# A float32 encoder layer on one core: 512-wide projection chunks, a ring of ten weight slices, an output projection summed by mixer, projection spread over all of the attention

## The reference

```python
h = x @ w_in                                   # 1024 -> 3328 columns, split below
qa, ka, va, ga, qb, kb, vb, gb = split(h)      # 512 512 512 512 | 512 128 128 512
# mixer A: 8 heads, rotary, sum of three dilated windows by a mask of log counts
# mixer B: 8 query heads on 2 key/value heads, q and k RMS-normalised, axial rotary
out_a = dilated_attention(rope(qa), rope(ka), va) * silu(ga)
out_b = attention(axial_rope(rms(qb)), axial_rope(rms(kb)), vb) * silu(gb)
f = concat(out_a, out_b) @ w_out
y = layer_norm(2 ** 0.25 * x + f, ln_g, ln_b)
```

## Time and profile before

| what | us |
|---|---|
| median of 3 runs (lowest, highest) | 476.59 (476.21, 477.52) |
| span of the profiled execution | 474.6 |
| PE busy, share of the span | 438.0, 92% |
| weight loads of PE | 413.2, 87% |
| DVE busy | 301.4, 64% |
| POOL busy | 248.1, 52% |
| ACT busy | 230.7, 49% |

### The profile page before, as it was taken

How to read it: one execution, slowest core, us unless ns; L and a number is a source line. 1 busy time by engine, 2 the same in 40 slices (tenths; PEclk the granted TensorE clock), 3 DMA queues, 4 the chain that set the end, 5 groups by cost and what they waited for, 6 DMA issues and landing times.

```text
span 474.6 us, 8965 instructions
## 1 busy us (share of the span) xinstructions
PE 438.0 (92%) x3292; PEld 413.2 (87%) x3292; DVE 301.4 (64%) x826; ACT 230.7 (49%) x519; POOL 248.1 (52%) x340
## 2 busy tenths in 40 slices
PE   1999979998899999999999999999999789999990
PEld 1999969987799999998899999999888678999990
DVE  1543675339987788664577877855586777433664
ACT  3332113335456565666565565655675876121222
POOL 1126953795554746334346565653543773454664
PEclk9999989999899999999999999999999989999997
DMA  6611212110200101102010010110200136231222
GB/s 237 255 45 52 71 35 74 39 46 23 68 23 23 46 23 36 56 24 66 14 54 23 24 46 24 40 51 23 68 1 23 44 111 245 88 95 42 78 100 89
DMA packets 23291, 30.00 MB, mean 63 GB/s; under 512 B 1872, under 2 KB 19408, under 8 KB 23248
## 3 DMA queue, kind: packets, MB, share of 16 engines
q1 hardware_dynamic: 22816, 29.30, 19.0%
q10 hardware_dynamic: 432, 0.13, 0.1%
HBM read 26.28 MB, written 3.15 MB: 62 GB/s over the span
## 4 chain that ended last, share of the span: by engine, by line
PE 66%; POOL 10%; DVE 10%; issue 7%; ACT 3%; DMA 2%; SPq 1%; ACTq 0%; DVEq 0%; POOLq 0%
PE bank L504 15%; PE bank L505 15%; PE bank L506 15%; PE bank L465 9%; PE bank L593 6%; POOL scr L1062 3%; DVE prob L870 2%; PE bank L551 2%; PE bank L552 2%; DMA h<-x_prompt 2%; DVE tmp_s L796 1%; POOL tanh L1048 1%; ACT prob L707 1%; DVE p_lo L878 1%; POOL w_lo L1032 1%
## 5 line engine op out<-in xcount | busy, mean ns | idle before, releaser
L504 PE MATMUL bank<-w_hi,t_lo 128*128 128x256 f32 x576 | 168.2, 292 | 1.9 <-DVE nmax L870 0.8
L506 PE MATMUL bank<-w_hi,t_hi 128*128 128x256 f32 x576 | 164.0, 285 | 0.0
L505 PE MATMUL bank<-w_lo,t_hi 128*128 128x256 f32 x576 | 163.9, 285 | 0.0
L504 PEld LDWEIGHTS bank<-w_hi,t_lo 128*128 128x128 f32 x576 | 111.5, 194 | 3.1 <-DVE nmax L870 1.0
L505 PEld LDWEIGHTS bank<-w_lo,t_hi 128*128 128x128 f32 x576 | 111.6, 194 | 0.1
L506 PEld LDWEIGHTS bank<-w_hi,t_hi 128*128 128x128 f32 x576 | 111.3, 193 | 0.0
L1032 POOL TENSOR_TENSOR w_lo<-raw,w_hi 128x512 fp32r<-128x512 f32 x52 | 67.2, 1302 | 59.2 <-ACT w_hi L659 59.1
L1113 POOL TENSOR_SCALAR prob<-prob,den 128x512 f32<-128x512 f32 (+1 forms) x96 | 60.5, 635 | 68.6 <-DVE den L899 68.5
L707 ACT ACTIVATE prob<-prob,nmax 128x512 f32<-128x512 f32 (+1 forms) x96 | 62.3, 649 | 54.1 <-DVE nmax L870 53.6
L878 DVE TENSOR_TENSOR p_lo<-bank,p_hi 128x512 fp32r<-128x512 f32 x80 | 54.8, 685 | 3.0 <-ACT p_hi L716 2.2
L659 ACT ACTIVATE w_hi<-raw 128x512 fp32r<-128x512 f32 x62 | 37.6, 622 | 34.6 <-DMA raw<-w_in 17.4
(11 more groups left out here) (97 smaller groups left out, 784.3 us busy)
## 6 DMA issues: line engine op xcount, KB each, us to landing
raw<-w_in SPq DMA_DIRECT2D x50, 256.0 KB, 2.8
raw<-w_out SPq DMA_DIRECT2D x16, 256.0 KB, 2.9
h<-x_prompt SPq DMA_DIRECT2D x7, 512.0 KB, 6.8
h<-x_sample SPq DMA_DIRECT2D x4, 512.0 KB, 9.6
y_prompt<-h SPq DMA_DIRECT2D x8, 256.0 KB, 2.1
y_sample<-h SPq DMA_DIRECT2D x4, 256.0 KB, 2.1
cst<-consts SPq DMA_DIRECT2D x1, 960.0 KB, 9.5
h<-x_prompt SPq DMA_DIRECT2D x2, 256.0 KB, 3.8
```

The source lines that it names most:

```text
L504: nc.tensor.matmul(out, a_lo, b_hi, start=(m == 0), stop=False)
L505: nc.tensor.matmul(out, a_hi, b_lo, start=False, stop=False)
L506: ins = nc.tensor.matmul(out, a_hi, b_hi, start=False, stop=(m == KT - 1))
```

## The change

Chunks of q, k (of mixer A) and of `w_out` become 512 columns wide; mixer A's q and k of four heads share one chunk (`X0`, `X1`). One matmul then streams 512 columns. A slice stays 256 KB, so a 512-wide chunk has eight slices of one row block, and the ring holds ten. The output projection is summed by mixer: `OB0`, `OB1` take the rows of mixer B and run inside steps 67 to 80, DVE adding them to the residual; `OA0`, `OA1` take mixer A's rows, and the first three row blocks of their first four items run in steps 81 to 83. Input items are cut into *atoms* (one row block, three passes) spread by cost over steps 0 to 66, half of a step's atoms before the transposes and half behind. Queries are transposed for two heads at once, with three places in `q_st`. Seventeen items come ahead of the attention: `KV` (6), `QB` (6), `GB0` (4) and one of `GB1`. Squares move from POOL to DVE, one norm is worked out per tile with its Newton operations, and tile n is normalised and rotated in the item behind it. `prepared` places each slice beside the atom that frees its ring place. The residual of x and the layer norm's parameters are loaded into parts of `h` as these come free.

Its core:

```diff
+SLOT = 512
...
+WIDTH = (256, 512, 256, 256, 512, 256, 256, 512, 256, 256, 512, 512, 512, 512)
...
+RING = 10
+RAW = 2
+FIRST = 4
...
-BESIDE = ((0, 5), (3, 8), (55, 44), (62, 50), (65, 52), (72, 54))
...
+ALONE = 14
+IN_STEPS, OB_STEPS, OA_STEPS = (0, 66), (67, 80), (81, 83)
+EARLY = 4
+EARLY_K = 3
...
+        k_tiles = [list(range(KT)) if c < IN_CHUNKS else list(range(KT // 2, KT)) if c in (OB0, OB1)
+                   else list(range(KT // 2)) for c in range(CHUNKS)]
+        items = [(c, n) for c in range(OA0) for n in range(parts[c])]
+        items += [(c, t) for t in range(TILES) for c in (OA0, OA1)]
...
+        def raw_before(g):
+
+            return g - RAW if g >= FIRST + RAW else g - FIRST
...
+        def slot_given_back(g):
+
+            c, s = slices[g]
+            if s == slice_count(c) - 1:
+                return acc_ready, index[(c, parts[c] - 1)] + 1
+            return slice_used, sum(slice_count(d) - 1 for d in range(c)) + s + 1
...
+        def spread(atoms, u0, u1):
+            total, so_far = sum(atom_cost(a) for a in atoms), 0
+            for a in atoms:
+                plan[u0 + so_far * (u1 - u0 + 1) // total].append(a)
+                so_far += atom_cost(a)
+
+        spread([a for i in range(AHEAD, IN_ITEMS) for a in atoms_of(i)], *IN_STEPS)
+        spread([a for i in range(IN_ITEMS, OA_ITEMS) for a in atoms_of(i)], *OB_STEPS)
+        spread([a for i in range(OA_ITEMS, OA_ITEMS + EARLY) for a in atoms_of(i, range(EARLY_K))], *OA_STEPS)
+        place_of = {a: i for i in range(AHEAD) for a in atoms_of(i)}
+        place_of.update({a: AHEAD + u for u in range(STEPS) for a in plan[u]})
+        finished = {u: [i for i in range(AHEAD, OA_ITEMS) if place_of[atoms_of(i)[-1]] == AHEAD + u]
+                    for u in range(STEPS)}
...
+        prepared = {p: [] for p in range(AHEAD + STEPS)}
+        at = 0
+        for g in range(slice_count(KV), len(slices)):
+            if g < RING:
+                at = (2, 3, 4, 4, 5, 5)[g - slice_count(KV)]
+            else:
+                c, s = slices[g - RING]
+                at = max(at, place_of[(index[(c, parts[c] - 1)], (s + 1) * per[c] - 1)])
+            prepared[at].append(g)
...
+        def rotations(place):
+
+            n = len(norms_of)
+            return {0: (), 1: (), 2: (0,), 3: (1, 2)}.get(place, (place - 1,) if place <= n else ())
...
+            for i in range(AHEAD):
+                if i + 1 < TILES:
+                    x_transposes(i + 1)
+                if i >= ALONE:
+                    t_batch(first[i - ALONE])
+                for _, m in atoms_of(i):
+                    accumulate(i, m)
...
+                before = (len(plan[u]) + 1) // 2
+                for i, m in plan[u][:before]:
+                    accumulate(i, m)
...
+                for i, m in plan[u][before:]:
+                    accumulate(i, m)
...
+            for i in range(AHEAD):
+                if i + 1 < TILES:
+                    x_high(i + 1, 0)
+                    x_high(i + 1, 1)
+                if i >= ALONE:
+                    t_high(first[i - ALONE])
+                for g in prepared[i]:
                     weights_high(g)
-                evacuate(0, t - 1)
-            evacuate(0, TILES - 1)
-            for c, n in alone:
-                for g in slices_at(c, n):
-                    weights_high(g)
-                evacuate(c, n)
-            for b, (c, n) in zip(first, first_items):
-                t_high(b)
-                for g in slices_at(c, n):
-                    weights_high(g)
-                evacuate(c, n)
+                evacuate(i)
...
+                if i == 2:
+                    tables()
+                for n in rotations(i):
+                    norm_and_rotate(n)
+                if KIND[items[i][0]] == NORM:
+                    sums(i)
+                evacuate(i)
...
-            def residual(c, t):
-
-                i = index[(IN_CHUNKS + c, t)]
-                r = h[:, t, c * CW:(c + 1) * CW]
+                for b in split_at[u]:
+                    mixed_low(b)
+            for b in splits[-2:]:
+                mixed_low(b)
+
+            def residual(i):
+                c, t = items[i]
+                n = c - OA0
+                r = res(t, n)
                 dve.wait_ge(acc_ready, i + 1)
-                after(nc.vector.scalar_tensor_tensor(out=r, in0=r, scalar=ALPHA, in1=accumulator(i)[:, 0:CW],
-                                                     op0=ALU.mult, op1=ALU.add))
-                nc.vector.bn_stats(stats[:, t, c, :], r).then_inc(dve_evacuated, 1)
-                if c == OUT_CHUNKS - 1:
+                after(nc.vector.tensor_tensor(r, r, accumulator(i)[:], ALU.add))
+                nc.vector.bn_stats(stats[:, t, n, :], r).then_inc(dve_evacuated, 1)
...
+            def head_rstd(n):
+                m = norm_heads(norms_of[n][0])
+                pool.wait_ge(summed, n + 1)
                 if n >= 2:
-                    pool.wait_ge(summed, n - 1)
...
+                v, y = ssq[:, n % 2, 0:m], scr[:, 0:m]
                 after(nc.gpsimd.tensor_scalar(v, v, 1.0 / HEAD_DIM, RMS_EPS, ALU.mult, ALU.add))
...
+                after(nc.gpsimd.tensor_tensor(y, v, half[:, 0:m], ALU.pow))
+                newton(rstd[:, n % 2, 0:m], v, y).then_inc(rstd_ready, 1)
+
+            def add_rotation(n):
+                c, t = ropes[n]
+                w = WIDTH[c] if c != KV else KV_WIDTH
...
+                r = h[:, t, HOME[c]:HOME[c] + w]
+                nc.gpsimd.tensor_tensor(r, r, tmp_s[:, n % 2, 0:w], ALU.add).then_inc(rope_added, 1)
```

More of the change, by code:

```diff
@@ L400, in group_of, with split_on_dve, split_taken @@
+        def split_on_dve(b):
+            return b[1] == 0 and b[0] in (3, 4, 6)
+        def split_taken(b):
+            n = splits.index(b)
+            return (mix_lo_dve if split_on_dve(b) else mix_lo_pool), \
+                sum(1 for d in splits[:n + 1] if split_on_dve(d) == split_on_dve(b))
         def group_of(u):
@@ L703, in exps @@
                 act.wait_ge(s_masked, u + 1)
-                rows = [(k, 0, SEQ)] if k < QT else [(QT + t, t * DEC_SEQ, (t + 1) * DEC_SEQ) for t in range(ST)]
-                for t, a, z in rows:
+                for t, a, z in rows_of(k):
                     s = prob[:, u % PRING, a:z]
@@ L1008, in _ @@
+            dve.wait_ge(ln_loaded, 32)
+            for i in range(OA_ITEMS, len(items)):
+                residual(i)
+                c, t = items[i]
+                if c == OA1 and t:
                     affine(t - 1)
```

885 lines of the change are left out of this document (409 added, 476 removed).

## The result

The changed kernel takes **593.5 us** (median of 4 runs, 591.6 to 594.3) against 476.4 of the kernel before: ratio 1.246 (95% interval 1.243 to 1.249). The forecast was 498, in a range of 470 to 514: the direction was right, the size was not. The profiled execution spans 592.2 us.

What follows compares the result with a forecast made beforehand. PE's matmul stream was taken as the bound. 474.6 less 8.3, 5.2, 8, 6 and 5.2 gave 441.9; plus opening 39.4, slices 8 and end 7.4 made a 496.7 us span, with 2.0 to the median 498, range 470 to 514.

Steps and rivals of the forecast that it cites:

- slices inside the attention: Attention: slices queue ahead of other work, but three steps of slack absorb most; 8 us lost, between nothing and 20.
- The sign for this case: Attention: long waits of PE at probability transposes around each slice burst would put the time over 506 us.
- The stream: PE's matmuls: 720 pairs merge into 512-wide ones, saving 8.3 us; 48 fewer transposes and a batch's start save 5.2.
- The estimate of 1.8 us: PE's matmuls: alternative saving of the 720 merges at a fixed 2.5 ns per matmul, not used in the sum.
- The end of the attention and 100 to 130: Output items filling steps 67 to 83 give back 8 us; norms moved ahead of 100 to 130 us give 6.
- The opening: Before the attention: slice queues and the norm loop delay item 14 by 36.2 us; 39.4 with low clock and trailing batches.
- first 9: Opening, item 7: PE waits because ACT copies item 5 only behind slice 13; 9 us lost, part of the 36.2.
- SP's loads at step 57: Attention, step 57: SP waits for a split of values, then issues seven loads ahead of slice 54; 2 us lost.
- The end: Last stage: PE waits 3.1 us for the last split, then layer norm sets the pace; 7.4 us lost, within 3 and 10.
- each burst shows: Attention: ACT and POOL, two thirds loaded, make PE wait at all nine slice bursts; 12 us more, 510 us; chance 0.15.

Runs made afterwards that it cites:

- e15: Changed kernel with ACT's old order restored, weight slices spread one to a step in the attention and a third raw buffer: 486.8 us.
- e13: Changed kernel with one thing undone, ACT's exponentials back behind the staging copies and the copy of the probabilities: 543.0 us.
- e9: Changed kernel with slices spread, third raw buffer, reordered opening, earlier rotation, and SP loading slices 54 to 56 and 62 to 64 ahead of residual loads: 506.1 us.
- e14: Kernel before the change with only ACT's exponentials moved ahead of the staging copy and the copy of the probabilities: 534.5 us, ratio 1.122.
- e3: Changed kernel with ACT, in the opening, copying the finished projection tile ahead of the high parts of slices 10 and later: 595.2 us.

## Why the prediction was wrong

**The step that failed** is the one on slices inside the attention, and one that is missing. "Three steps lie between a unit's scores and its transposes, so most is absorbed" is true of the exponentials and scalings, which I named as what queues behind the slices. It is not true of the copy of the probabilities of unit u - 3, which stands in the same queue and which PE needs by the next step. Slices were priced at 8 us with 20 as the worst; they cost 47 in the attention (56.1 less the 8.8 ahead of it). And the sum has no term for the move of the exponentials, 50.5 us. 39 and 50.5 make 90 of the 95.5 us by which the sum (496.7) missed the span (592.2); the other 6 stay open. The sign for this case that the prediction gave, long waits at the transposes of probabilities, was looked for in the wrong place: those waited 2.1 us in all, and the values behind them 42.2.

Point by point:
- *The stream.* Right in kind. The changed trace has 0.227 us between 512-wide starts in the opening and 0.231 in the attention, so the 720 merges save 5.5 to 8.3 us. The estimate of 1.8 us that the prediction worked out from the figure of the Trainium skill (page "TensorE: Matmul & The Clock Gate", section "Wait — 56ns, not 53.3ns?") would have been too low.
- *The end of the attention and 100 to 130* (14 us back): not seen in the changed kernel, where PE is busy for 72.8 of the 85.6 us of steps 67 to 83 (85%, over 90 forecast). In e15 PE is busy for 310.8 of 315.5 us of the attention, so these losses are gone once the queues allow it; the 14 us were not measured by themselves.
- *The opening.* 36.2 us forecast at item 14 and 37.5 measured (116.1 against 78.6 unhindered), by the mechanism given: the loop of norms (7.3 to 8.3 us a tile, 7.2 forecast; power 1.65, 1.9 forecast), slice 14, six slices on ACT, copy, norm, rotation. Only "first 9" was 8. That the total agrees so closely is in part luck: the power was 0.25 us cheaper than forecast and the loop still a little slower.
- *SP's loads at step 57*: forecast 2 us. In e13 steps 60 and 61 lose some 9 us, and putting the loads later brought 4.4 in e9.
- *The end*: forecast 3.1 us of wait and 39.9 from there. Measured 2.92, and 592.2 - 552.7 = 39.5:

```profile
552.70 0.47 PE L563 MATMUL bank<-w_hi,t_lo 128*128 128x512 f32 x1 [2.92 <-DVE t_lo L948]
```

- *The rival "each burst shows"* (0.15, 510) had the right mechanism and a third of the price (12 us more, where the groups cost 39 more): its loads of "two thirds" took ACT and POOL for independent servers. With 2.35 us for a slice and two buffers, a group of four does not fit a step of 3.7 us. Had I drawn the order of ACT for one step as I did for the opening, both terms would have been seen.

The low clock is part of these costs, not a further one. An estimate from the starts in the stretches at the lower clock, behind the first 17 us, in which both kernels are alike: matmuls at twice their distance cost some 34 us in the changed kernel and some 5 before. They follow long waits, here the one of 6.38 us at step 20, in rows of PE:

```profile
232.83 0.55 PE L638 MATMUL bank<-p_hi,v_st 128*128 128x256 f32 x1 [6.38 <-DVE p_lo L914]
...
234.68 0.63 PE L598 MATMUL bank<-k_lo,q_st 128*128 128x512 f32 x1
235.10 0.63 PE L599 MATMUL bank<-k_hi,q_st 128*128 128x512 f32 x1
...
236.02 0.28 PE L563 MATMUL bank<-w_hi,t_lo 128*128 128x256 f32 x1
236.14 0.28 PE L564 MATMUL bank<-w_lo,t_hi 128*128 128x256 f32 x1
```

The distance is 0.42 for 512 columns, at a granted clock of 0.50 (1.2 GHz), and 0.12 for 256 a little later, at 1.00 (2.4 GHz) again. This went into no term of mine for the attention. What remains open: e14 lost 58 us where the undoing gave 50.5 and 54.5; the parts of this difference are not known.

## What to carry to other kernels

Write down, for each engine, the order of one step, and mark for every hand-over the last instruction ahead of it in the same queue: if two engines wait for each other twice in a step, the order decides whether the waits overlap or add up to a loop, and a slower loop takes all that is hung on it. Read a diff for lines that only moved, as closely as for those that are new; here they cost more than anything I had priced. A group of loads behind two buffers holds up whatever stands behind it on each engine that touches the data, so taking it out of one queue alone can win nothing, as in the opening here (e3).

## What the runs showed of the hardware

- POOL's power takes 1.65 us for eight elements in each partition, beside 0.70 for two and 1.08 for four: 0.14 to 0.19 for each further element.
- A product of DVE with two operands in SBUF does not run beside a sum of POOL of the same kind. L936 takes 0.42 us mostly, and 1.15 to 1.30 in all eight places where POOL's L1074 had begun 0.3 to 0.4 us ahead of it; POOL and DVE of the changed kernel:

```profile
208.68 1.29 POOL L1074 TENSOR_TENSOR h<-h,tmp_s 128x512 f32<-128x512 f32 x1 [4.19 <-DVE h L843]
```

```profile
208.95 1.29 DVE L936 TENSOR_TENSOR mix_t<-o_lo,mix_t 64x256 f32<-64x256 f32 x1
```

It ends 0.27 us behind POOL's, and 0.27 to 0.30 in the other seven. The Trainium skill (page "SBUF — State Buffer", section "🔬 SBUF: two separate sides") describes the pair of ports that both share as an exclusive lock for the whole instruction; these rows agree.
